# Attention tiles on TensorE: float32 products of the two projections in halves of 64 stationary columns, of the router in quarters of 32, and the weighted sum with its head groups in turns

## The chip, the cores and the metric

One core of one Trainium2 chip runs the whole program. The metric is the device time of one execution in microseconds (us); lower is better. The engines are named as the profile names them: PE is TensorE (its weight loads are shown apart as PEld), DVE is VectorE, ACT is ScalarE, POOL is GpSimd, SP is SyncE, which here issues most of the DMAs.

## What is computed

One layer of a streaming encoder on x of 2048 tokens by 1024 features, in float32. After a conditioned RMSNorm, one product with W_in (1024 x 1280) gives queries (8 heads of 64), keys and values (2 heads of 64) and 512 pooling channels. Attention sees a window of two chunks of 64 tokens and a sink; beside it stand four moving averages. Both go through W_out (1024 x 1024). Then a second RMSNorm, a router to 128 experts (8 chosen of each token, by groups) and the mixture of experts with a shared expert.

```
h = modulate(rmsnorm(x, norm1_g), shift1, scale1)
proj = h @ w_in                       # q | k | v | u
a = sink_window_attention(q, k, v, attn_sinks);  p = multiscale_pool(u, pool_w, pool_scale)
x = x + gate1 * (concatenate([a, p]) @ w_out)
h2 = modulate(rmsnorm(x, norm2_g), shift2, scale2)
scores = sigmoid(h2 @ w_router)       # then the choice of 8 experts of each token
x = x + gate2 * (experts(h2, choice) + shared(h2));  return rmsnorm(x, final_g)
```

## The kernel before

The tokens are cut into 16 tiles of 128. The program has three parts: the products that make the conditioning vectors (line 951), a loop over the token tiles that does everything up to the routing (the attention part), and a loop over blocks of 128 token slots that does the experts. Each engine has its own program, written out by hand, and they meet by semaphores only. No scheduler moves anything: each engine runs its instructions in the order of the code.

The attention part is a software pipeline: `tiles` calls `step(i)` for i from -2 to 17, the middle twelve from a hardware loop. One step works on up to three tiles, since the first projection belongs to tile i+1, attention to tile i, and normalisation and routing to tile i-1. PE's step is, in this order:

- transposes of the normalised input of tile i+1 (line 956), which wait for DVE's `v_xn`
- scores of the heads of tile i (line 970): for each head and each chunk c one product with 64 rows of contraction and 64 stationary columns; output partitions 0 to 63 for c=0, 64 to 127 for c=1
- two small bf16 products for the ranks (lines 977 and 978)
- the first projection of tile i+1 (line 986): n over three PSUM banks (512, 512 and 256 columns of W_in), k over 8 pieces of the contraction, the transposed tile `xT[:, k, :]` stationary with 128 columns
- moving averages (lines 993 and 994), transposes of h2 (line 956) and of the attention weights (line 1002)
- the router (line 1011): 8 products with `h2T[:, k, :]` stationary, 128 columns of the router's weights moving. It waits for ACT's copy of h2T
- the weighted sum (line 1022, semaphore `p_pv`): for head group g_ and chunk c the values are stationary, 64 columns, and 256 columns of attention weights move; output partitions 0 to 63 for g_=0, 64 to 127 for g_=1
- the pooling product (line 1026, `p_py`), transposes of q and k (lines 1033 and 1034)
- the second projection (line 1045, `p_wo`): n over two banks, k over 8 pieces, `mixT[:, k, :]` stationary with 128 columns, 512 columns of W_out moving. It waits for DVE's `v_yT` (line 767)

DVE's step ends with the scaling of the pooling product (line 767, which waits for `p_py`), the choice of experts (lines 772 to 808, which needs ACT's exponential of the router's output), and the normalisation of the next input (lines 700 to 706, 813 and 814), which gives `v_xn`.

All operands of the changed products are float32. In the trace such a product leaves two MATMUL and two LDWEIGHTS records, here called its two passes. A transpose leaves one of each.

```
for n, w in ((0, 512), (1, 512), (2, 256)):
    for k in range(KD):
        last = mm(B[4 + n][:, 0:w], xT[:, k, :], w_in[:, k, n * 512:n * 512 + w], start=(k == 0), stop=(k == KD - 1))
```

Of the kernel before, what the change touches and what calls it, by code (L numbers as in the profile page):

```python
# [6 lines left out]
P = 128  # L7
T = 2048
D = 1024
KD = D // P  # L10
NT = T // P
HD = 64
# [8 lines left out]
E = 128  # L21
# [89 lines left out]
def build(nc, A, out):  # L111
# [4 lines left out]
    with ctx:  # L116
# [13 lines left out]
        def C(name):  # L130
            at, w = AT[name]
            return cst[:, at:at + w]
# [8 lines left out]
        w_in = W[:, 0:KD * IN].rearrange("p (k n) -> p k n", k=KD)  # L141
        w_out = W[:, 10240:18432].rearrange("p (k n) -> p k n", k=KD)
        w_rt = W[:, 24576:25600].rearrange("p (k n) -> p k n", k=KD)
# [14 lines left out]
        def take(*shape):  # L158
            n = int(np.prod(shape))
            a = S[:, cut[0]:cut[0] + n]  # L160
            cut[0] += n
            if len(shape) == 2:
                a = a.rearrange("p (a b) -> p a b", a=shape[0])
            return a
# [3 lines left out]
        xT = take(KD, P)  # L168
# [3 lines left out]
        h2T = take(KD, P)  # L172
        qkf = take((NH + 2) * HD)
        qk = qkf.rearrange("p (a b) -> p a b", b=HD)
        vC = take(KVW)
        vE = take(KVW)
# [7 lines left out]
        mixT = take(KD, P)  # L184
# [47 lines left out]
        B = [PB[:, n, :] for n in range(8)]  # L232
# [11 lines left out]
        def W8(eng, name, val):  # L244

            if isinstance(val, int) and val <= 0:
                return
            eng.wait_ge(s[name], val)

        def settle(eng):  # L250

            eng.sem_inc(s["settled"], 1)

        def ok(j):
            return not isinstance(j, int) or 0 <= j < NT
# [688 lines left out]
        def _(pe):  # L944
            mm, tr = nc.tensor.matmul, nc.tensor.transpose
            pe.wait_ge(s["v_cb"], 1)
            for m in range(12):
                pe.wait_ge(s[f"c_ada{m % NSTRIP}"], 32 * (m // NSTRIP + 1))
                W8(pe, "v_mod", m - 1)
                for k in range(KD):  # L950
                    last = mm(B[m % 2], cb[:, k, :], ada[m % NSTRIP][:, k, :], start=(k == 0), stop=(k == KD - 1))  # L951
                last.then_inc(s["p_mod"], 1)

            def transposes(banks, src, name):
                for k in range(KD):
                    last = tr(B[banks[k // 4]][:, (k % 4) * P:(k % 4 + 1) * P], src[:, k * P:(k + 1) * P], ident)  # L956
                last.then_inc(s[name], 1)

            def step(i):
                if ok(i + 1):  # L960
                    W8(pe, "v_xn", i + 2)
                    transposes((2, 3), xn, "p_xT")
                if ok(i):
                    W8(pe, "a_qkT", i + 1)
                    settle(pe)
                    for h in range(NH):
                        g_, j = h // 4, h % 4
                        rs = slice(HD * g_, HD * g_ + HD)
                        for c in range(2):
                            last = mm(B[g_][c * HD:(c + 1) * HD, j * P:(j + 1) * P], qT[rs, j, c * HD:(c + 1) * HD],  # L970
                                      kb[rs, c * P:(c + 1) * P], start=True, stop=True)
                    last.then_inc(s["p_sc"], 1)
                if ok(i - 2):
                    W8(pe, "v_mask", i - 1)
                    W8(pe, "v_c16", i + 1)
                    W8(pe, "v_rank", i - 2)
                    mm(B[6][:, 0:E], tri16, mask16, start=True, stop=True)
                    mm(B[6][:, E:2 * E], ones16, mask16, start=True, stop=True).then_inc(s["p_rk"], 1)
                if ok(i + 1):
                    W8(pe, "a_xT", i + 2)  # L980
                    W8(pe, "v_x1", i)
                    for n, w in ((0, 512), (1, 512), (2, 256)):
                        if n == 2:
                            W8(pe, "v_rank", i - 1)
                        for k in range(KD):
                            last = mm(B[4 + n][:, 0:w], xT[:, k, :], w_in[:, k, n * 512:n * 512 + w], start=(k == 0), stop=(k == KD - 1))  # L986
                    last.then_inc(s["p_proj"], 1)
                if ok(i):
                    W8(pe, "a_u", i + 1)
                    bd = C("band0") if isinstance(i, int) and i == 0 else C("band")  # L990
                    for g_ in range(NPG):
                        cs = slice(g_ * P, (g_ + 1) * P)
                        mm(B[7][:, cs], uC[:, cs], bd[:, cs], start=True, stop=False)
                        last = mm(B[7][:, cs], uP[:, cs], C("bandp")[:, cs], start=False, stop=True)
                    last.then_inc(s["p_bd"], 1)
                if ok(i - 1):
                    W8(pe, "v_h2", i)
                    transposes((2, 3), h2, "p_h2T")
                if ok(i):
                    W8(pe, "v_P", i + 1)  # L1000
                    for h in range(NH):
                        last = tr(B[h // 4][:, (h % 4) * P:(h % 4 + 1) * P], sc[:, h, :], ident)
                    last.then_inc(s["p_PT"], 1)
                if ok(i - 1):
                    W8(pe, "a_h2T", i)
                    W8(pe, "c_rest", 32)
                    if ok(i + 1):
                        W8(pe, "a_u", i + 2)
                    W8(pe, "v_rank", i - 1)
                    for k in range(KD):  # L1010
                        last = mm(B[6][:, 0:E], h2T[:, k, :], w_rt[:, k, :], start=(k == 0), stop=(k == KD - 1))  # L1011
                    last.then_inc(s["p_rt"], 1)
                if ok(i):
                    W8(pe, "a_PT", i + 1)
                    W8(pe, "c_wt", 80)
                    W8(pe, "v_PT", i + 1)
                    W8(pe, "a_v", i + 1)
                    W8(pe, "v_mx", i + 1)
                    O = B[0].rearrange("p (a b) -> p a b", a=4)
                    for g_ in range(2):  # L1020
                        for c, vv in ((0, vE), (1, vC)):
                            last = mm(O[g_ * HD:(g_ + 1) * HD, :, c * HD:(c + 1) * HD], vv[:, g_ * HD:(g_ + 1) * HD],
                                      PT[:, 4 * g_:4 * g_ + 4, c * HD:(c + 1) * HD], start=True, stop=True)
                    last.then_inc(s["p_pv"], 1)
                    for g_ in range(NPG):
                        last = mm(B[1][:, g_ * P:(g_ + 1) * P], poolw[:, g_, :], mx[:, g_, :], start=True, stop=True)
                    last.then_inc(s["p_py"], 1)
                if ok(i + 1):
                    W8(pe, "v_rope", i + 2)
                    W8(pe, "a_rt", i)  # L1030
                    W8(pe, "a_u", i + 2)
                    for k in range(4):
                        tr(B[6][:, k * P:(k + 1) * P], qkf[:, k * P:(k + 1) * P], ident)
                    last = tr(B[7][:, 0:P], qkf[:, 4 * P:5 * P], ident)
                    last.then_inc(s["p_qkT"], 1)
                if ok(i):
                    W8(pe, "a_aT", i + 1)
                    W8(pe, "v_yT", i + 1)
                    if ok(i + 1):
                        W8(pe, "a_qk", i + 2)  # L1040
                        W8(pe, "a_u", i + 2)
                        W8(pe, "a_v", i + 2)
                    for n in range(2):
                        for k in range(KD):
                            last = mm(B[4 + n], mixT[:, k, :], w_out[:, k, n * 512:(n + 1) * 512], start=(k == 0), stop=(k == KD - 1))  # L1045
                    last.then_inc(s["p_wo"], 1)

            pe.wait_ge(s["v_wo"], 1)
            pe.wait_ge(s["c_win"], 16)
            tiles(pe, step)  # L1050

            pe.wait_ge(s["e_cnt"], 1)
# [71 lines left out]
```

## Time and profile before

| | us |
|---|---|
| median of the 2 runs | 3495.68 |
| the two runs | 3494.86 and 3496.49 |
| span of the profiled execution, first to last instruction | 3472.9 |
| attention part, from about 170 to about 930 of the span | 760 |
| PE busy in these 760 us | 687.5 |
| DVE busy in them | 487.3 |
| mean granted PE clock in them | 0.95 |

The metric holds the launch and the end around the span too: 3495.68 - 3472.9 = 22.8 us lie outside it. Busy time of PE is the union of its matmul records, whose ends are modelled: a record lasts longer than the time until the next one starts, because products are pipelined. The granted clock is 1.00 at 2.4 GHz and 0.50 at 1.2 GHz.

### The profile page before, as it was taken

What the parts mean: (1) busy time and instruction counts of PE and PEld (TensorE: products, weight loads), DVE (VectorE), ACT (ScalarE), POOL (GpSimd) and SP (SyncE); (2) the same over time, 40 slices, a digit from 0 to 9 for tenths busy, and PEclk for the clock granted to TensorE, in tenths of its full rate; (3) what the DMA queues carried; (4) which work ended last, traced back from release to release, by engine and by line L of the source; (5) the groups of instructions that cost most, each with busy time, mean ns of one, the idle gap of its engine ahead of it and who ended that gap; (6) DMA issues with size and microseconds to landing.
All of it is one profiled execution on the core that took longest, in us unless ns stands there. A gap on an engine that the chain in (4) does not pass through costs nothing.

```text
span 3472.9 us, 61999 instructions
## 1 busy us (share of the span) xinstructions
PE 2951.9 (85%) x13151; PEld 2180.6 (63%) x13152; DVE 2164.1 (62%) x3443; ACT 1706.3 (49%) x2435; POOL 925.5 (27%) x794
## 2 busy tenths in 40 slices
PE   6699999999469989888798888888888888998883
PEld 2355555555358877776676767676767667776662
DVE  1146666666643665667676766666766675667774
ACT  0133333333133654656565655556556565656565
POOL 0001111111223333232333333333332323333331
PEclk9899999999779999999899999999999999999896
DMA  9501111111175887989998999899989998899997
GB/s 368 163 25 49 49 48 36 49 36 43 67 182 122 239 228 208 269 260 259 289 295 252 290 281 274 258 271 285 288 259 265 265 293 232 247 266 280 294 275 249
DMA packets 415300, 730.08 MB, mean 210 GB/s; under 512 B 31521, under 2 KB 297377, under 8 KB 414754
## 3 DMA queue, kind: packets, MB, share of 16 engines
q1 hardware_dynamic: 341314, 500.17, 42.5%
q0 software_dynamic: 73824, 228.47, 28.6%
q14 instruction: 149, 1.22, 0.1%
q8 instruction: 13, 0.21, 0.0%
HBM read 587.37 MB, written 141.19 MB: 210 GB/s over the span
## 4 chain that ended last, share of the span: by engine, by line
DMA 45%; PE 22%; issue 12%; DVE 8%; POOL 7%; POOLq 4%; ACT 2%; DVEq 0%; SPq 0%; ACTq 0%
DMA rec<-rec_tab 42%; PE PB L986 8%; POOL arena L461 3%; POOL acc_tab L492 3%; POOLq L476 3%; PE PB L951 2%; PE PB L1068 2%; PE PB L1070 2%; PE PB L1069 2%; DMA arena<-in_ada_b 1%; PE PB L1045 1%; PE PB L956 1%; DMA acc_tab<-arena,rec 1%; PE PB L970 1%; PE PB L1011 1%
## 5 line engine op out<-in xcount | busy, mean ns | idle before, releaser
L887 DVE TENSOR_TENSOR WS<-RAW,WS (+1 forms) x774 | 900.8, 1219 | 127.3 <-ACT WS L586 125.3
L586 ACT CAST WS<-RAW (+1 forms) x774 | 759.5, 1052 | 153.2 <-DMA RAW<-in_w_up_e 99.6
L1068 PE MATMUL PB<-WS,XR 128*128 x1720 | 685.6, 399 | 52.2 <-issue 46.6
L461 POOL DMA_INDIRECT arena<-h_tab,rec x219 | 255.3, 1166 | 1574.7 <-DMA rec<-rec_tab 1381.1
L1070 PE MATMUL PB<-WS,XR 128*128 x1720 | 674.7, 392 | 0.0
L1069 PE MATMUL PB<-WS,XR 128*128 x1720 | 674.0, 392 | 0.0
L917 DVE SCALAR_TENSOR_TENSOR arena<-PB,rec,G 128x512 f32<-128x512 f32 x430 | 302.5, 745 | 383.7 <-DMA acc_tab<-arena,rec 336.5
L1068 PE MATMUL PB<-WS,HR 128*128 x860 | 402.9, 468 | 154.1 <-DVE HR L921 153.0
L492 POOL DMA_INDIRECT acc_tab<-arena,rec x215 | 402.5, 1872 | 93.3 <-issue 68.4
L1068 PEld LDWEIGHTS PB<-WS,XR 128*128 128x128 f32 x1720 | 327.6, 190 | 158.7 <-issue 91.8
L1069 PEld LDWEIGHTS PB<-WS,XR 128*128 128x128 f32 x1720 | 326.7, 190 | 66.1
L1070 PEld LDWEIGHTS PB<-WS,XR 128*128 128x128 f32 x1720 | 325.4, 189 | 67.6
L1070 PE MATMUL PB<-WS,HR 128*128 x860 | 363.4, 423 | 0.0
L1069 PE MATMUL PB<-WS,HR 128*128 x860 | 361.6, 420 | 0.0
L956 PE MATMUL PB<-cst,arena 128*128 128x128 f32 x1984 | 265.4, 278 | 97.3 <-DVE arena L814 53.1
L449 POOL DMA_INDIRECT rec_tab<-recs,posi x128 | 124.6, 973 | 795.5 <-DVE recs L748 754.8
L956 PEld LDWEIGHTS PB<-cst,arena 128*128 128x128 f32 x1984 | 235.8, 143 | 138.2 <-DVE arena L814 48.4
L894 DVE TENSOR_TENSOR XR<-PB,XR 128x512 fp32r<-128x512 f32 x432 | 277.6, 684 | 65.0 <-ACT XR L590 64.8
L608 ACT ACT_TABLE_LOAD x215 | 275.8, 1283 | 74.4 <-issue 70.5
L1068 PEld LDWEIGHTS PB<-WS,HR 128*128 128x128 f32 x860 | 176.4, 205 | 193.0 <-issue 169.4
L986 PE MATMUL PB<-arena 128*128 128x512 f32 (+1 forms) x768 | 293.7, 544 | 1.5 <-ACT arena L515 1.2
L590 ACT ACTIVATE XR<-PB 128x512 fp32r<-128x512 f32 x432 | 234.6, 595 | 98.3 <-PE PB L956 98.3
(233 smaller groups left out, 2982.6 us busy)
## 6 DMA issues: line engine op xcount, KB each, us to landing
RAW<-in_w_gate_e SPq DMA_DIRECT2D x128, 1024.0 KB
RAW<-in_w_up_e SPq DMA_DIRECT2D x128, 1024.0 KB
RAW<-in_w_down_e SPq DMA_DIRECT2D x128, 1024.0 KB, 8.6
arena<-in_ada_w SPq DMA_DIRECT2D x12, 2048.0 KB, 14.3
arena<-in_x SPq DMA_DIRECT2D x32, 512.0 KB, 3.6
h_tab<-arena SPq DMA_DIRECT2D x17, 512.0 KB, 2.9
acc_tab<-arena SPq DMA_DIRECT2D x16, 512.0 KB, 2.6
out<-fa SPq DMA_DIRECT2D x16, 512.0 KB, 4.7
```

The lines of the kernel that those rows point to most:

```text
L461: g.indirect_dma_start(xg[n % AHEAD], None, h2_tab, bass.IndirectOffsetOnAxis(ap=rec[:, n % UNROLL, 0:1], axis=0)).then_inc(s[f"xg_r{n % A ...
L492: g.indirect_dma_start(acc_tab, bass.IndirectOffsetOnAxis(ap=rec[:, (n - 1) % UNROLL, 0:1], axis=0), ys[(n - 1) % 2], None, compute_op=ALU ...
L586: nc.scalar.copy(to, of).then_inc(s["a_hig" if k < 4 else "a_hid"], 1)
L608: A_(eg, B[7][:, 0:F], ACT.Silu).then_inc(s["eg_done"], 1)
L887: last = V.tensor_tensor(lo, raw, hi, ALU.subtract)
L894: V.tensor_tensor(xl[:, 4 * n:4 * n + 4, :], B[2 + n].rearrange("p (a b) -> p a b", a=4), xhf[:, 4 * n:4 * n + 4, :], ALU.subtract).then_i ...
L917: last = V.scalar_tensor_tensor(out=ys[(n - 1) % 2][:, c * 512:(c + 1) * 512], in0=B[4 + c], scalar=recf[:, (n - 1) % UNROLL, 1:2], in1=G2 ...
L956: last = tr(B[banks[k // 4]][:, (k % 4) * P:(k % 4 + 1) * P], src[:, k * P:(k + 1) * P], ident)
L986: last = mm(B[4 + n][:, 0:w], xT[:, k, :], w_in[:, k, n * 512:n * 512 + w], start=(k == 0), stop=(k == KD - 1))
L1068: mm(bank, hi[:, k, :], w(k, 0), start=(k == 0), stop=False)
L1069: mm(bank, hi[:, k, :], w(k, EW), start=False, stop=False)
L1070: last = mm(bank, lo[:, k, :], w(k, 0), start=False, stop=(k == K - 1))
```

## The change

Four edits, all in PE's step. The first projection is done for 64 stationary columns (tokens) and then for the other 64, with k inside. The router is done for four groups of 32 tokens, with k inside. The second projection alternates between the two halves of 64 at each k. The weighted sum has its two loops exchanged, so that output partitions 0 to 63 and 64 to 127 alternate. The waits, the buffers and the other engines' programs stay as they are; later lines move down by 1 to 3.

```
-                        for k in range(KD):
-                            last = mm(B[4 + n][:, 0:w], xT[:, k, :], w_in[:, k, n * 512:n * 512 + w], start=(k == 0), stop=(k == KD - 1))
+                        for r in (slice(0, HD), slice(HD, P)):
+                            for k in range(KD):
+                                last = mm(B[4 + n][r, 0:w], xT[:, k, r], w_in[:, k, n * 512:n * 512 + w], start=(k == 0), stop=(k == KD - 1))
...
-                    for k in range(KD):
-                        last = mm(B[6][:, 0:E], h2T[:, k, :], w_rt[:, k, :], start=(k == 0), stop=(k == KD - 1))
+                    for r in (slice(0, 32), slice(32, 64), slice(64, 96), slice(96, P)):
+                        for k in range(KD):
+                            last = mm(B[6][r, 0:E], h2T[:, k, r], w_rt[:, k, :], start=(k == 0), stop=(k == KD - 1))
...
-                    for g_ in range(2):
-                        for c, vv in ((0, vE), (1, vC)):
+                    for c, vv in ((0, vE), (1, vC)):
+                        for g_ in range(2):
...
                     for n in range(2):
                         for k in range(KD):
-                            last = mm(B[4 + n], mixT[:, k, :], w_out[:, k, n * 512:(n + 1) * 512], start=(k == 0), stop=(k == KD - 1))
+                            for r in (slice(0, HD), slice(HD, P)):
+                                last = mm(B[4 + n][r, :], mixT[:, k, r], w_out[:, k, n * 512:(n + 1) * 512], start=(k == 0), stop=(k == KD - 1))
```

On PE, in the hardware loop of the attention part, from the rank products to the moving averages, there stands before (the first number of a shape is the output's partitions, the second its columns; xN counts products):

```order
L977 MATMUL PB<-c16 128x128
L978 MATMUL PB<-c16 128x128
L986 MATMUL PB<-arena 128x512 x16
L986 MATMUL PB<-arena 128x256 x8
L993 MATMUL PB<-cst,arena 128x128
L994 MATMUL PB<-cst,arena 128x128
```

and now:

```order
L977 MATMUL PB<-c16 128x128
L978 MATMUL PB<-c16 128x128
L987 MATMUL PB<-arena 64x512 x32
L987 MATMUL PB<-arena 64x256 x16
L994 MATMUL PB<-cst,arena 128x128
L995 MATMUL PB<-cst,arena 128x128
```

The first projection has twice as many products, each for half the output partitions, at the same place. On PE, from the router to the end of the same step, there stands before:

```order
L1002 MATMUL PB<-cst,arena 128x128 x8
L1011 MATMUL PB<-arena 128x128 x8
L1022 MATMUL PB<-arena 64x4x64 x4
L1026 MATMUL PB<-arena,poolw 128x128 x4
L1033 MATMUL PB<-cst,arena 128x128 x4
L1034 MATMUL PB<-cst,arena 128x128
L1045 MATMUL PB<-arena 128x512 x16
```

and now:

```order
L1003 MATMUL PB<-cst,arena 128x128 x8
L1013 MATMUL PB<-arena 32x128 x32
L1024 MATMUL PB<-arena 64x4x64 x4
L1028 MATMUL PB<-arena,poolw 128x128 x4
L1035 MATMUL PB<-cst,arena 128x128 x4
L1036 MATMUL PB<-cst,arena 128x128
L1048 MATMUL PB<-arena 64x512 x32
```

The router has four times as many products and the second projection twice as many; nothing passes anything else. The weighted sum keeps its four products in another order among themselves.

## Rows read from the trace of the kernel before

**Rows 1.** The page: span.
```profile
span 3472.9 us, 61999 instructions
```

**Rows 2.** Windows: attention part, experts.
```profile
core 0: us, PE busy (x) PEld busy (x) DVE busy (x) ACT busy (x) POOL busy (x), PEclk, DMA share, GB/s
170.00:930.00 760.00, 687.46 (x2986) 406.29 (x2985) 487.27 (x1190) 252.76 (x501) 109.64 (x113) 0.95 0.13 44
...
990.00:3340.00 2350.00, 2076.68 (x9590) 1662.98 (x9589) 1550.11 (x1995) 1358.81 (x1790) 761.84 (x620) 0.96 0.90 260
```

**Rows 3.** Waits, 170 to 930 us: waiter <- releaser, total us, times, longest.
```profile
DVE arena L767 <- PE PB L1026: 60.1, 15, 4.1
PE PB L956 <- DVE arena L814: 29.0, 13, 2.2
PE PB L1045 <- DVE arena L767: 10.8, 15, 0.7
PE PB L1011 <- ACT arena L539: 9.0, 14, 0.6
```

**Rows 4.** PE's timeline of one step: start us, length us, line, form, count.
```profile
690.57 2.89 PE L970 MATMUL PB<-arena 64*64 64x128 f32 x32
...
714.06 1.04 PE L956 MATMUL PB<-cst,arena 128*128 128x128 f32 x8
714.94 1.04 PE L1002 MATMUL PB<-cst,arena 128*128 128x128 f32 x8
716.62 2.05 PE L1011 MATMUL PB<-arena 128*128 128x128 f32 x16 [0.64 <-ACT arena L539]
718.60 1.09 PE L1022 MATMUL PB<-arena 128*64 128x256 f32 x8
719.62 1.16 PE L1026 MATMUL PB<-arena,poolw 128*128 128x128 f32 x8
...
722.04 13.97 PE L1045 MATMUL PB<-arena 128*128 128x512 f32 x32 [0.72 <-DVE arena L767]
738.25 1.09 PE L956 MATMUL PB<-cst,arena 128*128 128x128 f32 x8 [2.23 <-DVE arena L814]
739.27 1.59 PE L970 MATMUL PB<-arena 64*64 64x128 f32 x32
```

**Rows 5.** Chain of waits over the same step: start us, length us.
```profile
716.62 2.05 PE PB L1011 x16
...
719.69 1.10 PE PB L1026 x8
...
721.08 0.86 DVE arena L767 x3
...
736.97 1.24 DVE arena L814
738.25 1.09 PE PB L956 x8
```

**Rows 6.** PE, 406 to 424.5 us, groups by form: busy us, mean ns.
```profile
L986 PE MATMUL PB<-arena 128*128 128x512 f32 x32 | 14.0, 594 | 0.0
L986 PE MATMUL PB<-arena 128*128 128x256 f32 x16 | 3.6, 379 | 0.0
```

**Rows 7.** Lines 1022 (all) and 970 (warm step): ns min/median/max, starts, form.
```profile
L1022 PE MATMUL PB<-arena x128: 379/379/430, 196.8 to 896.9; 128*64 128x256 f32 x128
L970 PE MATMUL PB<-arena x32: 269/269/320, 739.3 to 740.6; 64*64 64x128 f32 x32
```

**Rows 8.** Windows round a fall of the clock, columns as in rows 2.
```profile
686.30:689.60 3.30, 1.07 (x6) 0.47 (x5) 3.19 (x5) 0.00 (x0) 0.00 (x0) 1.00 0.00 0
689.80:693.00 3.20, 3.20 (x34) 2.87 (x35) 1.71 (x2) 2.22 (x5) 0.00 (x0) 0.50 0.62 220
693.20:696.40 3.20, 3.20 (x10) 1.47 (x7) 2.79 (x6) 0.98 (x1) 0.00 (x0) 0.50 0.20 83
696.60:700.00 3.40, 3.40 (x9) 1.52 (x8) 1.52 (x5) 2.29 (x5) 0.00 (x0) 1.00 0.00 0
```

**Rows 9.** The last tile's router, PE's timeline (the step at 1.2 GHz).
```profile
927.38 3.79 PE L1011 MATMUL PB<-arena 128*128 128x128 f32 x16 [1.18 <-ACT arena L539]
```

## The prediction

> **What bounds the kernel now.** I read the windows first, to see in which part the change lies. The attention part takes 760 us of the span of 3472.9 [rows 1, 2]. In it PE is busy for 687 us, 90%, and DVE for 487; the granted clock is 0.95. The expert part, 2350 us, is not touched, and starts when the attention part is done. So what a tile of the attention part gains or loses counts about 16 times, and the rest moves along. A gain or loss of 2%, about what a measurement of this kernel can tell from no change, is 70 us, or 4.4 us in each tile.
>
> Next the waits. PE waits little, and for three things: at the start of a step for DVE's last instruction (29.0 us in 13 waits), before the second projection for DVE's line 767 (10.8), before the router for ACT's copy (9.0) [rows 3]. DVE waits 60.1 us for PE's line 1026. Then the chain, to see which of PE's work lies on the path: from the router (716.62) over line 1026 to DVE's line 767, the choice of experts, the normalisation (line 814) and then PE's transposes of the next step at 738.25 [rows 5]. The second projection isn't in it: it starts at 722.04, its last record ends at 736.01, and PE then stands 2.23 us until line 814 is done [rows 4]. So the first projection, the router, the weighted sum and line 1026 are on the path; the second projection has 2.2 us to spare and would have to lose more than that to count.
>
> **What a narrow float32 product costs.** This decides everything. A product with 128 stationary columns runs its two passes one after the other: the second projection needs 13.97 us for 32 passes, whose last record lasts 0.59, so (13.97 - 0.59) / 31 = 0.43 us for a pass of 512 columns [rows 4, 6]. For 256 columns it is (3.6 - 0.38) / 15 = 0.215 [rows 6], for the router's 128 it is (2.05 - 0.275) / 16 = 0.111, taking 0.275 for the last record's tail [rows 4].
>
> Line 1022 shows the form with 64 stationary columns, 128 rows and 256 moving columns: 4 products, 8 passes, in 1.09 us [rows 4], with a last record of 0.38 [rows 7]. One after the other they would need 7 x 0.215 + 0.38 = 1.88 us. In pairs, the two passes of a product side by side, they need 3 x 0.215 + 0.38 = 1.03, and 0.06 more at the start. So a half product costs half of a full one, and two halves cost what the full one did.
>
> Do halves that write different output partitions overlap too? The scores alternate between the two output halves at every product, as the new second projection will [rows 4]. They are 16 products of 128 columns, in two groups of 64 rows. One pair of passes takes 0.43 / 4 = 0.11 us. All 16 in a line would take 15 x 0.11 + 0.27 = 1.9 us; seen are 1.59, that is (1.59 - 0.27) / 0.11 = 12 places [rows 4, 7]. That is what comes out if the two row groups overlap for half of their length and the products within a group follow each other. With the output halves side by side as well it would be 6 places and 0.9 us. In line 1022 too the change of half lies in the middle, and 1.03 us is the time with no overlap there. I take none.
>
> **First projection.** 16 full products of 512 columns and 8 of 256 become 32 and 16 half ones. Before 32 x 0.43 + 16 x 0.215 = 17.2 us; now 32 x 0.43 + 16 x 0.215 = 17.2. The form with 512 columns is not in the trace; the bounds are half of it (all overlaps) and twice (passes one after the other), and I take the value of the nearest row, line 1022, which differs only in the moving columns.
>
> **Second projection.** 16 products become 32: 32 x 0.43 = 13.8 us, as before. Its bounds are 6.9 and 27.5 us. Being shorter gains nothing, since line 814 comes last; that is worked out below.
>
> **Weighted sum.** The same four products, in turns: 0. If halves overlapped, 2 x 0.215 = 0.43 us less a tile, 7 us in all.
>
> **Changes of width.** Each time PE goes from one stationary width to another, some overlap is lost. From line 956 to 1002, same width, the next record starts 0.16 us before the last one's end (714.06 + 1.04 - 714.94); from 1011 to 1022 and from 1022 to 1026 it is 0.07 [rows 4]. So a change costs 0.09. The group behind it starts slower too: line 1026 takes 1.16 us for 8 passes where line 1002 takes 1.04, so 0.1, and line 1022 lost 0.06. New on the path are the changes into the first projection (0.09 + 0.06) and out of it (0.09 + 0.1): 0.34 us a tile, 16 x 0.34 = 5.4 us. Those before the router and at both ends of the second projection fall into waits that are there now (0.64, 0.72 and 2.23 us [rows 4]), and between router and weighted sum there is one already.
>
 The loss is on the path in full, since lines 1022, 1026 and DVE's 767 stand behind it, and then all of DVE's choice of experts; the second projection moves by the same amount and keeps its spare time. Fifteen tiles make 25.2 us. The last tile's router runs at 1.2 GHz and takes 3.79 us [rows 9]; at twice the times above, 31 x 0.22 + 0.54 = 7.3, 3.5 more.
>
> **Sum.** 25.2 + 3.5 + 5.4 = 34 us. On the profiled span that is 3472.9 + 34 = 3507; with the 22.8 us outside it, 3530, 1.0% over the median of 3495.7.
>
> **Rivals.**
> *The halves overlap.* The second projection would take 6.9 us. But the next step waits for line 814, whose chain starts at line 1026, so PE only stands longer: 2.2 + 6.9 = 9.1 us. And standing costs: after a gap of 2.2 us and more the granted clock went from 1.00 to 0.50, for some 6.8 us, and came back when the first projection had run for about 3 us [rows 8]. A fallen step start costs 2.89 - 1.59 = 1.3 us in the scores [rows 4] and about 4 passes at 0.86 for 0.43, 1.7 us: 3 us. At 0.95 the attention part has 760 x 0.05 x 2 = 76 us at half clock; about 30 of them lie at its two ends, so 46 / 6.8 = 7 of 14 starts are slow now. Seven more cost 21 us, the weighted sum gains 7: 3530 + 14 = 3544. Against it stands the count of places above. The Trainium skill says in "TensorEngine Tiling (Array Packing)", section "Key Properties", that tiles of the array operate independently, so that loads and products of different ones run in parallel. By that rule this rival would be right; the trace shows it for the row groups of the scores, not for their column halves.
>
> *The router costs nothing.* The narrow width pays back in full: 3530 - 28.7 = 3501. For it speaks that the step from 128 to 64 columns did so; against it that this step is explained by two passes, and there are no four.
>
> *The router's passes follow each other.* 15 x 5.2 + 10 + 5.4 = 94 us, 3590: slower by over 2%. Line 1022 speaks against it.
>
> *The clock stays down.* This is the one that ends far on the other side. At a step start PE stood, the clock fell, and 3.2 us of unbroken narrow products (the scores, 689.8 to 693.0) did not bring it back; it was back after the next 3.2 us, with wide products [rows 8]. After the change both projections are narrow. If those don't raise the clock, the first fall decides: the first projection costs 17.2 us more, the second 13.8 less its 2.2 to spare, the rest of PE's path about 5: 34 us a tile, for some 14 tiles 480 us, 4010 in all. Against it: the scores use 64 rows, the projections 128, and with their passes side by side, as in line 1022, PE is as unbroken at work in them as before.
>
> **How the numbers follow.** The forecast has 0.60, the free router 0.22, overlapping halves 0.06, the router's single passes 0.07, the clock that stays down 0.05. The likeliest case gives 3530. The range of 3496 to 3562 holds the first three with the measurement's spread and an unseen width change or clock fall in the middle of some steps; the two slow cases, 0.12, are outside. Both are slower by over 2%: 0.12. No case is faster by 70 us; 0.02 is for what I have not seen. That leaves 0.86 for within 2%.
>
> **What would show it.** In the changed profile: the first projection still near 17.4 us from first to last record, passes in pairs; the second at 13.9 to 14.1 us with PE still waiting about 2.2 us for line 814 behind it; the router 3.7 us in a step at full clock; the weighted sum still 1.09. Granted clock in the attention part near 0.95. A router of 2.0 or 7.3 us gives the second or third rival right; a second projection of 7 us and step starts that are all slow, the first; a clock far below 0.95, the last. A first projection that differs from 17.4 us by more than 1 us would break the main step of the sum.

## The result, and the profile after

The changed kernel takes 3722.57 us (median of 3716.86 and 3728.27) against 3495.68: 1.064 times, 95% interval 1.059 to 1.069. That is 227 us more, where 34 were forecast, and outside the range.

Where does it lie? The windows of the changed kernel, from the first scores (line 970) to the first rows of the experts (line 894), and from there to the end. So cut, the attention part is longer than the 760 us of the table, which stop at 930. The columns are those of [rows 2]:

```profile
181.00:1202.00 1021.00, 903.95 (x5003) 486.99 (x5001) 514.35 (x1283) 258.58 (x509) 129.22 (x133) 0.94 0.12 38
1202.00:3726.00 2524.00, 2139.46 (x9890) 1707.25 (x9890) 1622.06 (x2104) 1434.51 (x1898) 789.85 (x644) 0.95 0.88 256
```

and of the kernel before:

```profile
171.00:983.00 812.00, 691.68 (x3001) 409.30 (x3000) 513.76 (x1283) 257.99 (x509) 129.71 (x133) 0.92 0.15 48
983.00:3472.00 2489.00, 2146.65 (x9890) 1719.30 (x9890) 1624.65 (x2104) 1433.07 (x1898) 789.05 (x644) 0.94 0.89 260
```

The attention part is 209 us longer, and it starts 10 us later, since the first tile's projection stands ahead of it: 219 us. DVE is busy for the same 514 us in both, PE for 212 us more. The granted clock did not get worse (0.94 for 0.92). The experts are 35 us longer in this profile. They aren't touched, and lay between 2489 and 2525 us in all 20 profiles of this study, in no order by kernel, so I count that as spread. The medians, 227 us apart, hold 219 of the attention part and 8 of spread.

PE's timeline in two steps of the changed kernel at full clock, start and length in us (compare [rows 4]; the rows up to 569.54 are from one step, the others from another):

```profile
539.71 1.09 PE L956 MATMUL PB<-cst,arena 128*128 128x128 f32 x8 [2.26 <-DVE arena L814]
540.74 1.59 PE L970 MATMUL PB<-arena 64*64 64x128 f32 x32
...
542.47 27.14 PE L987 MATMUL PB<-arena 128*64 128x512 f32 x96
569.54 0.49 PE L994 MATMUL PB<-cst,arena 128*128 128x128 f32 x2
...
696.83 5.96 PE L1013 MATMUL PB<-arena 128*32 128x128 f32 x64 [0.65 <-ACT arena L539]
702.71 1.08 PE L1024 MATMUL PB<-arena 128*64 128x256 f32 x8
703.72 1.16 PE L1028 MATMUL PB<-arena,poolw 128*128 128x128 f32 x8
...
706.15 13.95 PE L1048 MATMUL PB<-arena 128*64 128x512 f32 x64 [0.72 <-DVE arena L767]
722.35 1.09 PE L956 MATMUL PB<-cst,arena 128*128 128x128 f32 x8 [2.25 <-DVE arena L814]
```

The first projection takes 27.1 us instead of 17.4, the router 5.96 instead of 2.05. The second projection (13.95), the weighted sum (1.08) and the spare time before line 814 (2.25) are as they were. 9.7 + 3.9 = 13.6 us a step, for 16 steps 218.

The difference between the two projections is the order. The weight loads of the first one show what PE does. Start and length in us; they are one load per row until the half changes:

```profile
546.39 0.14 PEld L987 LDWEIGHTS PB<-arena 128*64 128x64 f32 x1 [0.29 <-issue]
546.82 0.14 PEld L987 LDWEIGHTS PB<-arena 128*64 128x64 f32 x1 [0.29 <-issue]
547.25 0.14 PEld L987 LDWEIGHTS PB<-arena 128*64 128x64 f32 x1 [0.29 <-issue]
547.67 0.19 PEld L987 LDWEIGHTS PB<-arena 128*64 128x64 f32 x3 [0.29 <-issue]
548.11 0.19 PEld L987 LDWEIGHTS PB<-arena 128*64 128x64 f32 x2 [0.24 <-issue]
548.53 0.19 PEld L987 LDWEIGHTS PB<-arena 128*64 128x64 f32 x2 [0.24 <-issue]
549.02 0.14 PEld L987 LDWEIGHTS PB<-arena 128*64 128x64 f32 x1 [0.29 <-issue]
```

One load, so one pass, every 0.43 us: as long as a pass with 128 columns took, for half of the output. Only around the change from one half to the other (547.67) are there two in each 0.43 us, for about four passes; then one again. This gives theory A: **passes whose outputs lie in the same column group of the array follow each other; passes of different groups run side by side; and PE finds a pass of the other group only about four passes ahead.** Worked out for the first projection: 64 passes of 0.43 us and 32 of 0.215 are 34.4 us; four are saved at each of the changes of half (three with 512 columns, two with 256 or at the border), 3 x 4 x 0.43 + 2 x 4 x 0.215 = 6.9; that leaves 27.5, seen are 27.1. The router: 64 x 0.109 less 3 x 4 x 0.109, and 0.27 of tail, is 5.9; seen 5.96.

### The profile page after: what moved, and what is told of

It is laid out like the page before. It is cut to its first block, busy times and chain, and to the rows that moved or that the text cites. A ratio compares the mean times of both kernels' runs of the same rounds, so it can differ in the third digit from the quotient of the medians.

```text
span 3726.6 us, 66095 instructions
## 1 busy us (share of the span) xinstructions
PE 3168.6 (85%) x15199; PEld 2248.9 (60%) x15200; DVE 2162.0 (58%) x3443; ACT 1708.3 (46%) x2435; POOL 925.8 (25%) x794
## 4 chain that ended last, share of the span: by engine, by line
DMA 43%; PE 26%; issue 11%; DVE 7%; POOL 6%; POOLq 4%; ACT 2%; DVEq 0%; SPq 0%; ACTq 0%
DMA rec<-rec_tab 40%; PE PB L987 12%; POOL arena L461 3%; POOL acc_tab L492 3%; PE PB L1013 3%; POOLq L476 2%; PE PB L951 2%; PE PB L1071 2%; PE PB L1073 2%; PE PB L1072 2%; DMA arena<-in_ada_b 1%; PE PB L1048 1%; PE PB L956 1%; DMA acc_tab<-arena,rec 1%; PE PB L970 1%
## 5 line engine op out<-in xcount | busy, mean ns | idle before, releaser
L1071 PE MATMUL PB<-WS,HR 128*128 x860 | 397.8, 463 | 180.8 <-DVE HR L921 179.8
L987 PE MATMUL PB<-arena 128*64 128x512 f32 (+1 forms) x1536 | 449.6, 535 | 1.4 <-ACT arena L515 1.2
L1073 PE MATMUL PB<-WS,HR 128*128 x860 | 358.9, 417 | 0.0
L1072 PE MATMUL PB<-WS,HR 128*128 x860 | 357.6, 416 | 0.0
L987 PEld LDWEIGHTS PB<-arena 128*64 128x64 f32 x1536 | 182.6, 139 | 263.9 <-issue 232.5
```

The lines of the kernel that those rows point to most:

```text
L987: last = mm(B[4 + n][r, 0:w], xT[:, k, r], w_in[:, k, n * 512:n * 512 + w], start=(k == 0), stop=(k == KD - 1))
L1071: mm(bank, hi[:, k, :], w(k, 0), start=(k == 0), stop=False)
L1072: mm(bank, hi[:, k, :], w(k, EW), start=False, stop=False)
L1073: last = mm(bank, lo[:, k, :], w(k, 0), start=False, stop=(k == K - 1))
```

## Experiments

The kernel before was timed beside every set, and was not always as fast: 3559 us (medians of 13 runs) beside the first two sets, 3498 and 3497 (17 each) beside two others, 3542 (11 runs, 3505 to 3587) beside the fourth. Why is the third question below. All ratios are against the runs of the same set.

**Each part alone.** e1: the first projection alone as in the changed kernel (first part of the diff); e2: the router alone (second part); e3: the second projection and the weighted sum alone (last two parts).

> Only the first projection is changed, as in the changed kernel (64 stationary columns, the 8 pieces of the contraction inside). Theory A (passes whose outputs lie in the same column group of the array follow each other; passes of different groups run side by side, if PE can reach the other group's pass by looking about four passes ahead): 27.1 us for the projection in a step at full clock instead of 17.4, so 9.7 x 16 = 155 us more, 3650 us or about 4.5% over the kernel before. Theory of the prediction (the two passes of a narrow product run side by side): 17.4 us and no change. The expert part is not touched: if its extra 30 us in the changed kernel came with the change, it should be longer here too; if they are only its own spread, it may be anything from about 2480 to 2520 us.

> Only the router is changed, as in the changed kernel (four groups of 32 columns one after the other). Theory A: 64 passes of 0.109 us, less four at each of three changes of group, 5.95 us in a step instead of 2.05, 3.9 us more; for 15 steps 58 us, and about 7 us for the last one at the low clock: 3560 us, 1.9% over before. Theory of the prediction: 3.7 us in a step, 29 us in all, 3524 us.

> Only the second projection and the weighted sum are changed, both with halves in turns. Theory A: both halves are always at work, the second projection takes 13.95 us and the weighted sum 1.08 in a step, as before; within 5 us of the kernel before. A rival in which every narrow product costs something (a load, an issue, more instructions to fetch) expects 10 us or more over before.

Measured: e1 1.024 times (1.020 to 1.028), e2 1.019 (1.015 to 1.023), e3 1.003 (0.999 to 1.006). In e1 a full-clock step has

```profile
469.13 27.14 PE L987 MATMUL PB<-arena 128*64 128x512 f32 x96
```

and its attention part is 968.7 us, 156 more than in the first profile of the kernel before, as theory A has it; the time is only 94 us over the 3559 of its own set, because there the kernel before loses some 55 us that e1 does not (below). Over the 3495.68 of the first runs, without such losses, it is 158 us. e2 is 69 us over, where 65 were expected by A and 29 by the prediction's theory. That it fits A so well is in part luck: the router took 5.95 us, A's number, in the first of its 16 tiles alone. In the next 13 it took 7.6 to 8.7; they suffer from the same losses as the kernel before beside it. (The last two tiles have a slow router in every kernel of this study.) The clean evidence for the router is the changed kernel, with 5.95 or 5.96 us in 14 of 16 steps. e3 is 7.7 us over, where 5 were allowed, but its ratio of 1.003 can't be told from 1. So the 227 us are those of two parts, and the two parts in which the halves take turns are free.

**The same product count, another order.** e4 is the changed kernel with the loops of the first projection and of the router exchanged, so that groups take turns at each piece of the contraction:

```
-    for r in (slice(0, HD), slice(HD, P)):
-        for k in range(KD):
+    for k in range(KD):
+        for r in (slice(0, HD), slice(HD, P)):
...
-    for r in (slice(0, 32), slice(32, 64), slice(64, 96), slice(96, P)):
-        for k in range(KD):
+    for k in range(KD):
+        for r in (slice(0, 32), slice(32, 64), slice(64, 96), slice(96, P)):
```

> The changed kernel, but with the groups of columns taking turns in the first projection (two halves at each piece of the contraction) and in the router (four quarters at each piece). Theory A: all groups of the array are at work at any time, the first projection takes 17.4 us again and the router 2.05 (64 passes of 0.109 us, four at a time, 1.75 and the tail 0.3); the time is that of the kernel before within 10 us. If only two groups can be at work at a time, the router takes 3.8 us: 28 us over before. Theory of the prediction (narrow products have a price of their own, order does not matter): as the changed kernel.

Measured: 1.006 (1.002 to 1.010), 21 us over before where at most 10 were expected. The changed kernel again (a_after_again) has 1.046 in the same set, 162 us over. PE's timeline of an early step of e4:

```profile
213.42 17.41 PE L987 MATMUL PB<-arena 128*64 128x512 f32 x96 [0.19 <-DVE arena L714]
...
235.20 1.95 PE L1013 MATMUL PB<-arena 128*32 128x128 f32 x64 [0.64 <-ACT arena L539]
...
240.52 13.95 PE L1048 MATMUL PB<-arena 128*64 128x512 f32 x64 [0.72 <-DVE arena L767]
```

The same 96 and 64 passes as in the changed kernel, in 17.41 and 1.95 us. The router's 64 passes in 1.95 us are 16 places of 0.109: four groups at a time. But this is the one step of e4 in which the router ran so. In the next 13 it took 3.45 to 6.54 us, in some at a granted clock of 0.50 (one of 3.64 us), in others broken up by gaps. These and the 21 us that stay are the subject of e13.

e7 is the opposite: the second projection, which was free, loses its turns (r outside, k inside).

> Only the second projection is changed, in halves of 64 columns but with all pieces of the contraction of one half before the other half. Theory A: 64 passes of 0.43 us less four at each of three changes of half, about 22.5 us instead of 14; 2.2 us of the 8.5 more were PE's spare time before DVE's line 814, so 6.3 us a step, 100 us in all over the kernel before in the same runs. Theory of the prediction: 14 us, no change. Rival (the price of one-sided order belongs to the first projection's place or operands): no change.

```profile
407.92 22.67 PE L1046 MATMUL PB<-arena 128*64 128x512 f32 x64 [0.72 <-DVE arena L767]
430.53 1.09 PE L956 MATMUL PB<-cst,arena 128*128 128x128 f32 x8
```

22.67 us instead of 13.97, and the wait behind it is gone: 1.028 (1.024 to 1.032), 96 us over; expected were 100. So the second projection had some 2 us to spare and no more. The close fit hides a gain that nobody had counted: where PE no longer stands at the start of a step, its clock no longer falls. In the kernel before the scores take 1.59 us, their time at full clock, in 7 of 16 steps, in e7 in 15. Its attention part is 89 us longer; 16 x 8.7 less the 29.0 of waits [rows 3] is 110, and eight slow starts fewer, at the prediction's estimate of 3 us each, leave 86.

**How far ahead, and what counts as the same.** In e5 the halves take turns every four products; in e6 all products of one half come first, but two PSUM banks take turns within it (the third bank's products stay 128 columns wide):

```
+    for k0 in range(0, KD, 4):                       # e5
+        for r in (slice(0, HD), slice(HD, P)):
+            for k in range(k0, k0 + 4):
...
+    for r in (slice(0, HD), slice(HD, P)):           # e6
+        for k in range(KD):
+            for n in range(2):
+                mm(B[4 + n][r, :], xT[:, k, r], w_in[:, k, n * 512:n * 512 + 512], ...)
```

> Only the first projection is changed: the halves take turns every four products (eight passes). Theory A with a look-ahead of four passes at each change of half (as the changed kernel's trace shows it): the last four passes of one group of products run beside the first four of the next, so all but four at each end are in pairs: 17.4 + 1 to 2 us, within 35 us of before. If each change of half gave only a fixed gain and the rest stayed in a line, with 11 changes instead of 5: 27.1 - 6 x 4 x 0.3 = about 20 us, 40 us over before. If order at this scale did not matter: 27.1 us.

> Only the first projection is changed: all products of the first 64 tokens, then all of the other 64, but for each piece of the contraction the two PSUM banks of 512 columns take turns; the third bank's 256 columns stay with 128 stationary columns. Theory A (what counts is the column group of the output): 64 passes of 0.43 us less four at the one change of half, 25.8 us, and 3.5 for the third bank: 29.3 us instead of 17.4, 12 us more in a step, 190 us in all. Rival B (passes follow each other because they add to the same PSUM addresses as the pass before, and would run side by side when they do not): 17.4 us or a little more, 0 to 20 us in all.

A step of e5, and one of e6:

```profile
270.64 19.63 PE L988 MATMUL PB<-arena 128*64 128x512 f32 x96
```

```profile
299.15 26.02 PE L985 MATMUL PB<-arena 128*64 128x512 f32 x64
325.10 3.72 PE L988 MATMUL PB<-arena 128*128 128x256 f32 x16
```

e6: 26.0 us for the 64 passes, 25.8 expected by A, 13.9 by the rival; 1.037 (1.034 to 1.041). It is 134 us over the kernel before of its set, but 197 over the first runs, where 190 were expected; like e1, it has none of the losses that its neighbour had. Another bank doesn't help, so it is not the adding to the same addresses. e5: 19.6 us, 2.2 more than in turns and a little more than A's 18.4 to 19.4. Counted as before, with four passes saved at each of 11 changes, it is 34.4 - 15.5 = 18.9; so "four" is good to about half a pass, and my rival of about 20 us, which counted in the same way, is not told apart from A. Only 27.1 us, order of no account, is ruled out. Its time missed my bound: 1.018 (1.010 to 1.026), 62 us over before for 35 of projection. The rest are stalls: ACT and DVE start late there on PE's results (56.7 us at line 533, 42.0 at line 760), and then the router runs at the low clock, in 13 of the first 14 tiles at 3.5 to 3.8 us for 2.05.

**Why the kernel before was not always as fast.** b and b2 are its profiles beside later sets, a the changed kernel's.

> The kernel before, unchanged, to see its profile in these later runs, where its median was 3559 us instead of 3496. Theory S (a stall): in most steps DVE's copy of the attention weights (line 762) starts 4 to 5 us late although PE's transposes for it are done, until the burst of 8 indirect DMAs of POOL (line 449) is over, as the profiles of e2_router_only and e3_second_and_sum show it; then the attention part takes about 872 us from the first line 970 to the first experts' line 894, instead of 812.7. Rival: the attention part is as before, 813 us, and the 60 us lie in the experts.

> The changed kernel, unchanged. Its first projection is 10 us longer, so POOL's burst is over before the transposes start. Theory S: no stall, attention part 1021 us as in its first profile; where the kernel before has the stall the ratio is about (3722 + 15) / 3559 = 1.05, where it has not, 1.064. Rival (a slower chip): both kernels are longer by the same 60 us, ratio 1.063.

In b the attention part takes 866.6 us, not 812.7, with the same instructions. In the step shown PE's transposes (lines 956 and 1002) are done at 429.2, but the copies of their results start at 433.6. DVE, ACT, POOL and PE there, with the idle time in brackets ("remote" is a release that the profile cannot tie to an instruction):

```profile
431.13 0.97 POOL L449 DMA_INDIRECT rec_tab<-recs,posi  x1 [0.30 <-issue]
...
433.59 0.60 ACT L538 ACTIVATE arena<-PB 128x512 f32<-128x512 f32 x1 [2.96 <-remote]
433.68 0.69 DVE L762 COPY arena<-PB 128x512 f32<-128x512 f32 x1 [3.67 <-remote]
...
434.73 3.53 PE L1011 MATMUL PB<-arena 128*128 128x128 f32 x16 [5.49 <-ACT arena L539]
```

DVE's line 762 waits so 13 times, 59.7 us in all; in the first profile never. It happens while POOL issues its burst of eight indirect DMAs (line 449). The router of this step takes 3.53 us for 2.05, since by then the clock has fallen: PE stood for 5.5 us, and the granted clock behind it is 0.50.

```profile
434.70:436.20 1.50, 1.47 (x7) 1.48 (x8) 0.00 (x0) 0.46 (x1) 0.00 (x0) 0.50 0.00 0
```

A burst beside short products isn't enough for it: in the first profile of the kernel before, the burst ran beside the transposes and the router as well (in one step from 375.6 to 385.6, the router at 380.98), and nothing waited. In the changed kernel the burst is over before the first projection ends. a shows none of the waits at line 762, and only one other, of 11 to 13 us, in the last tiles: attention part 1025.7 us, 4.5 more than in its first profile. So its ratio is 1.046 (1.036 to 1.055) there and 1.064 where the kernel before has no stalls. e9 holds the burst back:

```
                 if ok(i - 2):
                     W8(g, "v_recs", i - 1)
+                    if ok(i):
+                        W8(g, "p_py", i + 1)
```

> The kernel before, but POOL's burst of 8 indirect DMAs waits for the pooling product (p_py), so that it runs beside the second projection instead of beside the transposes and the router. Theory S: the stalls of 4 to 5 us a step are gone, attention part 813 to 820 us where it is 867 to 872, about 50 us less than the kernel before in the same runs. Rival: the stall comes from something else than the burst; no change, or the burst stalls the second projection instead.

In that set the kernel before had no stalls (3498 us), and e9 had 1.000 (0.997 to 1.002): no answer. So it was run again:

> The kernel before, unchanged, for its profile beside the next runs. Either the attention part is about 813 us and DVE's line 762 starts at once (no stalls), or about 867 us with 13 waits of 4 to 5 us.

> The kernel before with POOL's burst of 8 indirect DMAs held back until the pooling product is done. If the kernel before shows the stalls in these runs and the burst is their cause: about 50 us less than before, attention part 813 to 820 us. If before shows none: no change, and it stays open. If before shows them and this kernel too: the burst is not the cause, or it stalls whatever stands beside it.

Now e9 takes 3486 us against 3542, 0.987 (0.982 to 0.991); that is 55 us less by the medians and 47 by the ratio, as the kernel before spread most in this set. Its attention part is 811.9 us with none of those waits. POOL's burst runs beside the second projection, whose length stays:

```profile
432.98 0.97 POOL L451 DMA_INDIRECT rec_tab<-recs,posi  x1 [35.82 <-PE PB L1028]
433.43 13.97 PE L1047 MATMUL PB<-arena 128*128 128x512 f32 x32 [0.72 <-DVE arena L769]
```

So the place of the burst decides: moved away from the short products, it stalls nothing. b2 fitted neither expectation: an attention part of 817.2 us, but waits called "remote" all the same, 51.3 us at ACT's line 546, 35.4 at DVE's line 762. There PE stood ahead of the second projection, which took 15.5 us and more in 8 of 16 steps but has time to spare, and then started most steps at full clock (first projection 17.4 us in 15 of 16), which made up for the waits. What in the chip couples burst and copies, and why it shows in some sets only, stays open. Each set ran on another chip, so chip and moment are not told apart.

**The router's quarters in turns, alone,** for a step without and one with the burst:

> Only the router is changed, in quarters of 32 columns that take turns at each piece of the contraction. Theory A: four passes at a time, 16 places of 0.109 us, 2.0 us in a step, within 5 us of before in all. If only two groups can be at work at a time: 3.8 us in a step, 28 us over before.

```profile
235.07 1.96 PE L1012 MATMUL PB<-arena 128*32 128x128 f32 x64 [0.65 <-ACT arena L539]
282.50 1.06 PE L1012 MATMUL PB<-arena 128*32 128x128 f32 x27 [0.79 <-ACT arena L539]
284.16 0.42 PE L1012 MATMUL PB<-arena 128*32 128x128 f32 x4 [0.60 <-issue]
284.89 0.27 PE L1012 MATMUL PB<-arena 128*32 128x128 f32 x1 [0.30 <-issue]
...
288.45 1.69 PE L1012 MATMUL PB<-arena 128*32 128x128 f32 x25 [0.34 <-issue]
```

Without the burst 1.96 us as expected, but that is one step of 16. With it the row breaks up after 27 passes, with gaps in which PE waits for nothing that the profile shows, and lasts over 7 us, as in eight of the steps: 1.014 (1.009 to 1.019), 38 us over by the medians. My bound of 5 us in all was missed. Many short passes suffer more from the burst than few. e13 puts all four edits in turns, as e4, with the burst held back, as e9.

> All four edits with the groups of columns in turns (as e4), and POOL's burst held back until the pooling product is done (as e9). Theory: order and stalls are the whole cause, so PE's steps are as long as before: router 1.96 us instead of 2.05, first projection 17.4, attention part 811 to 816 us, whatever the runs are like; the time of e9 within 5 us. Rival (narrow products cost something of their own, by their four times as many instructions): 10 us or more over that, in the attention part.

```profile
431.83 1.95 PE L1015 MATMUL PB<-arena 128*32 128x128 f32 x64 [0.64 <-ACT arena L541]
```

Measured: 1.0015 (0.9995 to 1.0035), attention part 815.3 us, no such waits, the router at 1.95 or 1.96 us in 14 of 16 steps. The kernel before had 812.7. So narrow products in turns cost next to nothing by themselves. That e4's 21 us were the stalls follows from e4's own profile, with its 13 long routers. e13 could not show it: in its set the kernel before had no stalls (3497 us), and a set with stalls was not tried.

**A version that is faster than both.** While reading the chain I saw that the pooling product stands behind the router and the weighted sum, and that DVE's line 767, and all of the choice of experts behind it, waits for it. e8 moves it ahead:

```
+                if ok(i):
+                    W8(pe, "c_wt", 80)
+                    W8(pe, "v_mx", i + 1)
+                    for g_ in range(NPG):
+                        last = mm(B[7][:, g_ * P:(g_ + 1) * P], poolw[:, g_, :], mx[:, g_, :], start=True, stop=True)
+                    last.then_inc(s["p_py"], 1)
                 if ok(i - 1):
                     W8(pe, "a_h2T", i)
...
+                    W8(pe, "v_yT", i + 1)
                     last = tr(B[7][:, 0:P], qkf[:, 4 * P:5 * P], ident)
```

(DVE's line 767 then reads bank 7.) e10 is e8 and e9 together.

> The kernel before with the pooling product moved ahead of the router, into PSUM bank 7, so that DVE's line 767 no longer waits behind router and weighted sum; the transposes of k wait for line 767 instead. The chain to DVE's line 814 gets shorter by about 2.4 us a step, and the second projection starts about 1 us earlier: 15 x 2.0 to 2.4 = 30 to 36 us less than before. Rival: the stall that POOL's burst causes now hits the pooling product and takes it back, 0 to 15 us less.

> The kernel before with the pooling product ahead of the router, again. Without stalls 54 us less than before, as measured. With stalls: between 20 and 54 us less.

> Both moves together: pooling product ahead of the router, POOL's burst behind it (it waits for p_py, which comes earlier now, so that the burst starts beside the router). If the stall needs the burst beside PE's short products, part of it is back: between 30 and 85 us less than the kernel before in the same runs. If the burst harms only the transposes: 80 us less.

> Pooling product early and POOL's burst behind it, again. Attention part about 756 us as in its first profile, whether or not the kernel before shows stalls beside it; 60 us less than before without stalls, 90 to 105 less with them. If the burst, which now starts beside the router, stalls it: attention part over 780 us.

```profile
709.37 1.04 PE L1002 MATMUL PB<-cst,arena 128*128 128x128 f32 x8
710.24 1.06 PE L1008 MATMUL PB<-arena,poolw 128*128 128x128 f32 x8
711.14 1.97 PE L1017 MATMUL PB<-arena 128*128 128x128 f32 x16
...
715.72 13.97 PE L1049 MATMUL PB<-arena 128*128 128x512 f32 x32 [0.90 <-ACT arena L554]
729.94 1.09 PE L956 MATMUL PB<-cst,arena 128*128 128x128 f32 x8 [0.25 <-DVE arena L814]
```

This is e8. The pooling product now fills PE's wait before the router, which follows at once, and the wait for line 814 is 0.25 us instead of 2.23. e8: 0.984 (0.981 to 0.987), 54 us less, more than the 36 expected. The rest is the clock. Before and in e8, without the last two tiles:

```profile
171.00:870.00 699.00, 648.84 (x2815) 381.98 (x2815) 447.50 (x1101) 239.83 (x480) 100.94 (x104) 0.96 0.12 43
172.00:870.00 698.00, 657.77 (x2971) 388.92 (x2972) 489.59 (x1190) 251.58 (x501) 108.58 (x112) 0.98 0.13 47
```

The granted clock is 0.98 for 0.96, and the scores take 1.59 us in 15 of 16 steps for 7. By the prediction's own estimate of 3 us for a slow start of a step, eight fewer are 24 us; with the 30 to 36 expected that makes 54 to 60, and the attention part is 59 us shorter (753.6 us). Beside stalls e8 has 0.988 (0.984 to 0.993), 47 less by the medians, in the range given, but 13 waits each at lines 762, 767 and 546, and an attention part of 812.2 us. e10: 0.984 (0.981 to 0.987) and 0.985 (0.982 to 0.988), 3437 and 3443 us, attention part 755.8 and 753.8. In both of its sets the kernel before had 3497 to 3498 us, so whether e10 gains 90 us beside stalls wasn't seen. Without stalls it is as fast as e8 within the spread. Both are faster than the kernel before clear of noise, by some 1.6%.

## Why the prediction was wrong

*What bounds the kernel*: right. The attention part took nearly all of the difference, the first projection and the router are on the path in full, and the second projection had 2.2 us to spare: e7 lost 96 us where 8.7 us more a step less 2.2, for 15 steps, are 98. That it fits to 2 us is luck: counted in full it is 86 (see e7), against an attention part that is 89 us longer.

*What a narrow float32 product costs*: this step failed, and the rest hung on it. I read line 1022 (8 passes of 256 columns in 1.09 us) as "the two passes of a product run side by side". The row has two readings that give the same number. Its order was four passes for output partitions 0 to 63, then four for 64 to 127. With a look-ahead of four passes the two sets of four run side by side, 4 x 0.215 + 0.2. A pass with 64 columns is as long as one with 128 (0.43 us at 512 columns, in the loads above), and the saving came from the other half. The scores had the same two readings: they alternate at every product, so 16 passes of one row group on two column groups take the same 8 places as 8 pairs. I had named both rows as evidence against overlapping halves; by A they are made by it, and e7 and the changed kernel bear A out on rows that have only one reading. Line 1022 never had more than four passes of one half in a row, and the new first projection has sixteen. The reading should have been tried on exactly that difference.

*First projection*: forecast 17.2 us, with bounds of half and twice. It was 27.1, 9.7 more, 155 us in all. I had the upper bound in the text and made no rival of it, so the range did not reach there.

*Router*: forecast 3.73 us, seen 5.96, between the forecast and the upper bound of 7.3. That is 2.2 us more a step than forecast, some 35 us. The rival "the router's passes follow each other", which had 0.07, was the nearest: they do, but for four at each of the three changes of group. "Line 1022 speaks against it" was the same misreading.

*Second projection and weighted sum*: 13.8 and 1.09 forecast, 13.95 and 1.08 seen, e3 within 0.3%. The numbers were right by the wrong reason: taking turns is what keeps them there.

*Changes of width*: not measured alone. The first record pair behind the projection lasts 0.49 us for 0.38, as assumed. 16 x 13.6 = 218 us of the 219 are accounted for by the two lines, so they are at most a few us.

*Rivals*. The halves do overlap, but that has no gain here: a pass of a half is as long as a full one, so overlap only brings the time back to what it was. The Trainium skill's "TensorEngine Tiling (Array Packing)", "Key Properties", has tiles work independently and in parallel. The runs bear that out for column groups too: four groups of 32 in 16 places (1.95 us), which the prediction had denied. The clock stayed up: 0.946 over the whole span for 0.935, and it came back during the narrow first projection, which was slow (28.8 us and more for 27.1) in 8 of 16 steps, as before (18.3 and more for 17.4).

*The sum*. The forecast put 22.8 us outside the span. The changed kernel's profiled execution shows 3728.27 us for a span of 3726.6, so 1.7 us lie outside, and the profile before was of a run about 21 us faster than the two timed ones. That moved no difference between the kernels, but it is the size of the spread.

## What to carry to other kernels

Splitting the stationary operand into column groups makes no pass shorter: the time comes back only if the passes of different groups take turns within about four passes, so put the loop over groups inside the loop over the contraction. When a row supports a cost by "n things in that time", write down every pairing that gives the number and ask which of them the new order keeps. And a wait that a product's place in the order causes (here the pooling product behind the router) may be worth more than any reshaping of products: 54 us for one move, of which some 20 come from a clock that no longer falls while PE stands.

## What the runs showed of the hardware that I had not expected

- Passes of float32 products to the same column group were one after the other in all runs (0.43 us at 512 moving columns, 0.109 at 128, at full clock), also with two PSUM banks in turns (e6), and the look-ahead to another group is about four passes (27.1 us for runs of 16, 19.6 for runs of 8, 17.4 in turns).
- Four groups of 32 columns work at the same time: 64 passes in 1.95 us (e13, 14 of 16 steps).
- Beside a burst of eight indirect DMAs from POOL, the copies that read PE's short products start 4 to 5 us late in some sets of runs and not at all in others, and PE's clock falls meanwhile (granted 0.50, router 3.5 us for 2.05); beside the long products of the second projection the burst does no harm (e9 again: 55 us less by the medians).
- A wait of 2.2 us at the start of a step costs more than itself: without it (e7, e8) the scores ran at full clock in 15 of 16 steps, with it (the kernel before) in 7.
